# Layer 1 of a two-layer transformer pair: gate tiles as fp32 matmuls between the recurrent steps, first attention beside the recurrent weight tiles, 24 modulation dots at the output projections

## What is computed

```python
mod = silu(c) @ w_ada + b_ada                      # 6 vectors of 1024: sh1, sc1, gt1, sh2, sc2, gt2
xn = rms_norm(h, norm1_g) * (1 + sc1) + sh1
q, k, v, zrw, gate_logits = split(xn @ w_in)       # 512, 512, 512, 1792, 2048 columns
o_moba = attention(rope(rms_norm(q)), rope(rms_norm(k)), v)     # 8 heads of 64, causal
o_rwkv = rwkv7_time_mix(token_shift(zrw), ...)     # 8 heads of 64, recurrent over the tokens
g_moba, g_rwkv = split(sigmoid(gate_logits))
mixed = g_moba * (o_moba @ w_proj_moba) + g_rwkv * (o_rwkv @ w_proj_rwkv)
h = h + gt1 * (mixed @ w_out)
xn2 = rms_norm(h, norm2_g) * (1 + sc2) + sh2       # then peer_ffn(xn2), then layer 2
```

## Time and profile before

| | us |
|---|---|
| median of 3 runs | 1953.65 (1952.32 to 1954.14) |
| the profiled execution | 1950.17 |
| its span, first to last instruction | 1948.4 |
| `w_in`, split tiles | from 57.3 to 173 |
| attention of layer 1 ends | 194.4 |
| recurrent part ends, `proj` starts | 390.8 |
| `w_out` starts | 422.8 |

### The profile page before, as it was taken

The page is one execution under the profiler, slowest core; times in us unless marked ns, Lnnn a source line. Parts: engine busy times, 40 slices in busy tenths (PEclk is TensorE's granted clock), DMA queues, the critical chain, the costliest instruction groups (busy, mean ns, idle before and its releaser), DMA issues.

```text
span 1948.4 us, 30492 instructions
## 1 busy us (share of the span) xinstructions
PE 1723.4 (88%) x10498; PEld 1505.8 (77%) x10498; DVE 1355.6 (70%) x2735; ACT 740.4 (38%) x1289; POOL 91.9 (5%) x107
## 2 busy tenths in 40 slices
PE   2998378697997998899999999999799997879997
PEld 2997367586986776788888888888699855669997
DVE  6888855424599996678888888888444635448886
ACT  1454300102411334455555555555244214414443
POOL 0001100000000000000000000000005302200000
PEclk8999789898998998999999999999899997989999
DMA  9895000043464115777777777777354370025653
GB/s 337 286 322 175 0 1 1 1 120 118 148 188 146 41 55 170 219 227 239 237 233 238 235 239 234 237 233 226 127 178 152 116 246 1 9 91 183 183 182 108
DMA packets 101164, 315.66 MB, mean 162 GB/s; under 512 B 11232, under 2 KB 20448, under 8 KB 100576
## 3 DMA queue, kind: packets, MB, share of 16 engines
q1 hardware_dynamic: 100512, 311.07, 50.1%
q10 hardware_dynamic: 576, 3.59, 0.5%
HBM read 309.11 MB, written 5.51 MB: 161 GB/s over the span
## 4 chain that ended last, share of the span: by engine, by line
PE 65%; DVE 21%; issue 7%; ACT 4%; DMA 2%; POOL 1%; DVEq 0%; SPq 0%; ACTq 0%; POOLq 0%
PE bank L462 7%; PE bank L463 7%; PE bank L464 7%; PE bank L477 4%; PE bank L1509 4%; PE bank L1550 4%; PE bank L1552 4%; PE bank L1554 4%; PE bank L438 3%; ACT whi L451 3%; PE bank L478 2%; PE bank L488 2%; DVE wlo L456 2%; PE bank L1314 2%; DVE xn L1662 1%
## 5 line engine op out<-in xcount | busy, mean ns | idle before, releaser
L456 DVE TENSOR_TENSOR wlo<-wring,whi 128x1024 fp32r<-128x1024 f32 x364 | 443.5, 1224 | 126.0 <-ACT whi L451 116.4
L451 ACT CAST whi<-wring 128x1024 fp32r<-128x1024 f32 x380 | 396.8, 1046 | 72.5 <-PE bank L1554 49.0
L462 PE MATMUL bank<-xboth,whi 128*128 128x256 f32 x1088 | 311.9, 287 | 24.2 <-DVE wlo L456 22.0
L463 PE MATMUL bank<-xboth,whi 128*128 128x256 f32 x1088 | 309.7, 285 | 0.0
L464 PE MATMUL bank<-xboth,wlo 128*128 128x256 f32 x1088 | 309.6, 285 | 0.0
L477 PE MATMUL bank<-xboth,whi 128*128 128x512 f32 x658 | 235.8, 397 | 0.0
L462 PEld LDWEIGHTS bank<-xboth,whi 128*128 128x128 f32 x1088 | 210.8, 194 | 27.0 <-issue 23.9
L463 PEld LDWEIGHTS bank<-xboth,whi 128*128 128x128 f32 x1088 | 210.9, 194 | 0.5 <-issue 0.5
L464 PEld LDWEIGHTS bank<-xboth,wlo 128*128 128x128 f32 x1088 | 210.8, 194 | 0.0
L478 PE MATMUL bank<-xboth,wlo 128*128 128x256 f32 x658 | 184.5, 280 | 0.0
L1550 PE MATMUL bank<-whi,Whi 128*128 128x512 f32 x512 | 161.0, 396 | 15.2 <-DVE Wlo L1645 15.2
(11 more groups left out here) (362 smaller groups left out, 2790.7 us busy)
## 6 DMA issues: line engine op xcount, KB each, us to landing
wring<-in_w SPq DMA_DIRECT2D x463, 512.0 KB, 3.7
arena<-in_ada SPq DMA_DIRECT2D x48, 512.0 KB, 5.0
xn<-in_ada SPq DMA_DIRECT2D x96, 256.0 KB, 3.2
h_spill<-arena SPq DMA_DIRECT2D x34, 128.0 KB, 1.7
arena<-h_spill SPq DMA_DIRECT2D x34, 128.0 KB, 3.6
wring<-in_w SPq DMA_DIRECT2D x6, 384.0 KB, 3.1
wring<-in_w SPq DMA_DIRECT2D x9, 256.0 KB, 2.6
arena<-in_const ACTq DMA_DIRECT2D x1, 1200.0 KB, 5.1
```

The lines of the kernel that those rows point to most:

```text
L451: act.copy(whi[:, n % HSLOTS, :], wring[:, n % SLOTS, :]).then_inc(hi_ready, 1)
L456: eng.tensor_tensor(wlo[:, n % SLOTS, :], wring[:, n % SLOTS, :], whi[:, n % HSLOTS, :].bitcast(F32), ALU.subtract).then_inc(lo_ready, 1)
L462: pe.matmul(out, h, xh, start=start, stop=False, **kw)
L463: pe.matmul(out, h, xl, start=False, stop=False, **kw)
```

## The change

**Order of `w_in`.** The phase `w_in` has 26 tiles now: v, q and k, then the recurrent ones. The 16 gate tiles are a phase of their own, `gates1`, behind it, and are not split: `pe_gates1` multiplies a block of 128 x 128 by 256 tokens as one fp32 matmul, 128 of them in all, put between steps of the recurrent part; `act_gates1` takes the sigmoids there.

**Attention.** The three small steps stand behind tiles 12, 14 and 16. Attention starts behind tile 18, and each of its first seven turns is followed by one of the tiles 19 to 25 on PE, ACT and DVE. Its PSUM banks are 3 and 4 (scores), 5 and 6 (transposes) and 7 (values), one bank for values.

**Dots.** Eight dots stay in `w_in`. The other 24 are done one or two at a time behind each of the 16 tiles of `proj` and `w_out`, with five buffers of their own; SP issues their loads between those of the tiles.

```diff
-PHASES = [("w_in", 42), ("proj", 8), ("w_out", 8), ("wq", 16), ("peer", 2 * NK),
+PHASES = [("w_in", 26), ("gates1", 16), ("proj", 8), ("w_out", 8), ("wq", 16), ("peer", 2 * NK),
...
+        MOBA_BANKS, LAYER2_BANKS = ((3, 4), (5, 6), (7,)), ((0, 1), (3, 4), (6, 7))
...
             def values(j):
                 n, g = j["n"], j["group"]
                 pe.wait_ge(a_pt, n + 1)
-                if j["first"] and g >= 2:
-                    pe.wait_ge(a_free, g - 1)
+                held = len(j["banks"][2])
+                if j["first"] and g >= held:
+                    pe.wait_ge(a_free, g - held + 1)
...
+        dots_before = lambda j: min(max(3 * j // 2, 0), 3 * KT)
+        def sp_layer1_out(sp):
+            def ada(i):
+                if i >= BSLOTS:
+                    sp.wait_ge(ada_used, 3 * KT + i - BSLOTS + 1)
+                sp.dma_start(aringb[:, i % BSLOTS, :], a["ada"][3 * KT + i]).then_inc(blanded[i % BSLOTS], 16)
+            sp.wait_ge(t_new, 20)
+            for i in range(BSLOTS):
+                ada(i)
+            for j, n in enumerate(range(FIRST["proj"], FIRST["peer"])):
+                sp.wait_ge(tile_done, n - SLOTS + 1)
+                sp.dma_start(wring[:, n % SLOTS, :], a["w"][n]).then_inc(landed[n % SLOTS], 16)
+                for i in range(dots_before(j - SLOTS) + BSLOTS, dots_before(j - SLOTS + 1) + BSLOTS):
+                    if i < 3 * KT:
+                        ada(i)
...
-            ring_tiles_split(pe, "w_in", 4, MB_SUMS_AT)
+            ring_tiles_split(pe, "w_in", 4, 13)
             pe_moba_sums(pe)
-            ring_tiles_split(pe, "w_in", MB_SUMS_AT, MB_GIVE_AT)
+            ring_tiles_split(pe, "w_in", 13, 15)
             pe_moba_give(pe)
-            ring_tiles_split(pe, "w_in", MB_GIVE_AT, MB_ROT_AT)
+            ring_tiles_split(pe, "w_in", 15, 17)
             pe_moba_turn(pe)
-            ring_tiles_split(pe, "w_in", MB_ROT_AT, 42)
+            ring_tiles_split(pe, "w_in", 17, ATT_TILE - 3)
+            pe.wait_ge(mb_q, 3)
+            att_pe(pe, moba_jobs, beside=lambda t: t + ATT_TILE < COUNT["w_in"] and
+                   ring_tiles_split(pe, "w_in", t + ATT_TILE, t + ATT_TILE + 1))
+        ATT_TILE = 22
...
+            lo_tile(15)
+            dve_shift(dve, v, 1)
+            dve_moba_given(dve)
+            lo_tile(16)
+            dve_shift(dve, v, 2)
+            lo_tile(17)
+            dve_shift(dve, v, 3)
+            lo_tile(18)
+            dve_shift(dve, v, 4)
+            dve_moba_turned(dve, v)
+            lo_tile(19)
+            dve_shift(dve, v, 5)
+            att_dve(dve, v, moba_jobs, beside=beside)
...
+        def pe_gates1(pe, n0, n1):
+            for n in range(n0, n1):
+                t, k = divmod(n, KT)
+                tile, r = FIRST["gates1"] + t, RING0["gates1"] + t
+                if k == 0:
+                    pe.wait_ge(landed[tile % SLOTS], count_at(tile))
+                    pe.wait_ge(ring_free, r - BANKS + 1)
+                mm = pe.matmul(bank[r % BANKS][:, 0:S], blocks(tile % SLOTS, k), xn[:, k, :],
+                               start=(k == 0), stop=(k == KT - 1))
+                if k == KT - 1:
+                    mm.then_inc(tile_done, 1)
...
         def pe_rwkv(pe):
+            pe_gates1(pe, 0, 8)
             pe.wait_ge(lora_loaded, 16)
...
             mm.then_inc(rw_ss, 1)
+            pe_gates1(pe, 8, 48)
             pe.wait_ge(bd_ready, 1)
...
+            pe_gates1(pe, 48, 64)
             pe.wait_ge(t_init, 4)
...
                     product(n + 2)
+                if n < 16:
+                    pe_gates1(pe, 64 + n, 65 + n)
...
                 mm.then_inc(q_u, 1)
+                pe_gates1(pe, 80 + 6 * c, 82 + 6 * c)
                 pe.wait_ge(q_us, c + 1)
...
                 mm.then_inc(q_sa, 1)
+                pe_gates1(pe, 82 + 6 * c, 84 + 6 * c)
                 pe.wait_ge(q_sas, c + 1)
...
                 mm.then_inc(q_y, 1)
+                pe_gates1(pe, 84 + 6 * c, 86 + 6 * c)
...
             mm.then_inc(gn_ss, 1)
+            pe_gates1(pe, 104, 128)
...
+            act_gates1(act, 1, 6)
             act.wait_ge(bd_ready, 1)
...
+            act_gates1(act, 6, 10)
+            act.wait_ge(t_new, 20)
+            act.dma_start(rB["crow"], a["crow"][0:1, :].to_broadcast([P, D])).then_inc(crow_loaded, 16)
...
                 dve.tensor_tensor(mix1[:, m, :], mixt[:, m % 2, 0, :], mixt[:, m % 2, 1, :], ALU.add).then_inc(ring_free, 1)
+                dve_late_ada(dve, m)
...
-            dve_residual(dve, "w_out", 2)
+            dve_residual(dve, "w_out", 2, beside=lambda m: dve_late_ada(dve, KT + m))
             norm_squares(dve, nsq[1])
+            dve.wait_ge(ada_used, 6 * KT)
+            dve_add_bias(dve, v, 3 * KT, 6 * KT)
```

More of the change, by code:

```diff
@@ L53 @@
 WIDTH = {"cmp_w2": 512, "uq": 768, "uk": 512, "uv": 512}
-RINGED = ["w_in", "proj", "w_out", "wq", "w_in2", "uq", "uk", "uv", "w_o"]
+RINGED = ["w_in", "gates1", "proj", "w_out", "wq", "w_in2", "uq", "uk", "uv", "w_o"]
 RING0 = {}
@@ L548, in spans, with turns @@
             return CAUSAL if job["kind"] == "causal" else CMP
-        def turns(jobs, *stages):
+        def turns(jobs, *stages, beside=None):
             first, last = jobs[0]["n"], jobs[-1]["n"]
@@ L556, in turns, with score_bank, turn_bank, value_bank @@
                         stage(jobs[t + ahead - first])
-        def att_pe(pe, jobs):
+                if beside:
+                    beside(t - first)
+        MOBA_BANKS, LAYER2_BANKS = ((3, 4), (5, 6), (7,)), ((0, 1), (3, 4), (6, 7))
+        def score_bank(j):
+            return bank[j["banks"][0][j["n"] % 2]]
+        def turn_bank(j):
+            return bank[j["banks"][1][j["n"] % 2]]
+        def value_bank(j):
+            return bank[j["banks"][2][j["group"] % len(j["banks"][2])]]
+        def att_pe(pe, jobs, beside=None):
             def scores(j):
-                n, bk = j["n"], bank[j["n"] % 2]
+                n, bk = j["n"], score_bank(j)
                 if n >= 2:
@@ L596, in values, with att_act @@
                 mm.then_inc(a_out, 1)
-            turns(jobs, (3, scores), (0, turn), (-1, values))
-        def att_act(act, jobs):
+            turns(jobs, (3, scores), (0, turn), (-1, values), beside=beside)
+        def att_act(act, jobs, beside=None):
             def exps(j):
@@ L619, in copy, with att_dve @@
                 if j["kind"] == "causal":
-                    ins = act.copy(buf["pt"][:, o:o + 384], bank[3 + n % 2][:, 0:384])
+                    ins = act.copy(buf["pt"][:, o:o + 384], turn_bank(j)[:, 0:384])
                 else:
-                    ins = act.copy(buf["pt"][0:NCMP, o:o + 256], bank[3 + n % 2][0:NCMP, 0:256])
+                    ins = act.copy(buf["pt"][0:NCMP, o:o + 256], turn_bank(j)[0:NCMP, 0:256])
                 ins.then_inc(a_pt, 1)
-            turns(jobs, (2, exps), (0, copy))
-        def att_dve(dve, v, jobs):
+            turns(jobs, (2, exps), (0, copy), beside=beside)
+        def att_dve(dve, v, jobs, beside=None):
             def maxima(j):
@@ L655, in output @@
                     dve.wait_ge(a_out, j["n"] + 1)
-                    dve.tensor_copy(j["out"], bank[6 + j["group"] % 2][j["rows"], 0:S]).then_inc(a_free, 1)
-            turns(jobs, (3, maxima), (1, reciprocals), (-2, output))
+                    dve.tensor_copy(j["out"], value_bank(j)[j["rows"], 0:S]).then_inc(a_free, 1)
+            turns(jobs, (3, maxima), (1, reciprocals), (-2, output), beside=beside)
         def att_pool(pool, jobs):
@@ L673, in build_layer_pair @@
         qr = rM["qn"].rearrange("p (m t) -> p m t", m=8)
-        moba_jobs = [dict(n=h, group=h, first=True, last=True, kind="causal", scale=MD ** -0.5, gate=None,
+        moba_jobs = [dict(n=h, group=h, banks=MOBA_BANKS, first=True, last=True, kind="causal", scale=MD ** -0.5, gate=None,
                           q=[qr[:, h // 2, :]], k=[kz[:, h, :]], M=128, buf=att1,
@@ L841, in act_w_in @@
+        def act_w_in(act):
+            for t in range(ATT_TILE - 3):
+                act_w_in_tile(act, t)
+                if t == 12:
                     act_moba_roots(act)
+            act_lora(act)
+            att_act(act, moba_jobs, beside=lambda t: t + ATT_TILE < COUNT["w_in"] and act_w_in_tile(act, t + ATT_TILE))
         mb_sq, mb_ss, mb_rt, mb_qn, mb_rot, mb_q = (sem("mb_sq"), sem("mb_ss"), sem("mb_rt"), sem("mb_qn"),
@@ new lines, in dve_w_in @@
+            lo_tile(12)
+            squares(1)
+            dve.wait_ge(ada_used, 3 * KT)
+            dve_add_bias(dve, v, 2 * KT, 3 * KT)
+            lo_tile(13)
+            lo_tile(14)
+            dve_shift(dve, v, 0)
+            dve.wait_ge(mb_rt, 1)
+            dve.reciprocal(mrt[:, 0:S], mrt[:, 0:S]).then_inc(mb_inv, 1)
+            lo_tile(15)
[4 more added lines that the diff above has]
+            lo_tile(17)
@@ L1337, in dve_residual @@
                 ins.then_inc(ring_free, 1)
+                if beside:
+                    beside(m)
```

(6 more changed lines are left out.)

139 lines of the change are left out of this document (69 added, 70 removed).

## The result

The changed kernel takes 1906.9 us, the median of four runs from 1904.19 to 1915.75; the kernel before, run beside it, takes 1953.89 us. The ratio is 0.9766, with a 95% interval from 0.9737 to 0.9794: faster by 2.3%. The forecast was 1911 us and a range from 1902 to 1923. The profiled execution of the changed kernel took 1909.39 us, its span is 1907.56 us; before these were 1950.17 and 1948.38. So the two traces differ by 40.8 us.

A forecast was written before the change was run, and what follows sets the result against it. PE was taken to bound the first stage and the projections, and mostly to wait for DVE in the recurrent part. Terms -46.1 - 0.2 + 0.3 + 2.8 - 1.0 - 1.5 + 2.3 + 0.8 = -42.6 us gave 1911 us, range 1902 to 1923.

The forecast's parts named there:

- Gate tiles, removed: First stage: sixteen split gate tiles, 2.88 us apart on PE, leave the path: -46.1 us.
- Gate tiles, added: Recurrent part: 128 gate matmuls of 0.436 us, mostly hidden in PE's gaps; +0.3 ahead of lora products, +2.8 in chunks.
- Attention: Attention among split tiles: idle terms +1.1, +1.4, +2.2, +3.3; last turns end 8.6 us behind tile 25, attention at 147.6.
- Interleaving moves the idle time but hardly lessens it: Attention's turns between split tiles: 8.0 us idle against 8.2 before, -0.2 us.
- The fifth rival: Attention was to overlap, but the sum already has that at -0.2; only the gates pay. No chance listed.
- Dots: `proj` and `w_out`: dots hidden except the last two ahead of the norm's squares, +2.3 us; DMAs 0, at most +6.
- Clock: PE's clock behind shortened gaps: updates -1.0 us, `proj` -1.5, norm +0.8.
- the chained turns: Attention turns with tiles: waits on ACT or DVE hold up the next turn, +12 us, 1923; chance 0.13.
- rival 2: Clock at its upper end everywhere, first unit included, and half of attention's 8.0 us idle gone: -9 us, 1902; chance 0.13.

The follow-up runs named there:

- the block of gates: Changed kernel with all 128 gate matmuls and 16 sigmoids in one block ahead of the lora products, none in gaps, updates or chunks: 1958.92 us.
- DVE's output first: Changed kernel with DVE copying out head t-2's values ahead of, not behind, the maxima of head t+3 in the first attention: 1905.29 us, ratio 0.9744.
- three edits: Changed kernel with DVE copying values out ahead of the maxima, chunk gates moved into the two long gaps, and dots spread over `proj` and `w_out`: 1898.28 us, ratio 0.9707.

## Why the prediction was right

The mechanism of the gain, whole gate tiles moved into gaps that hold them, and most terms were as put, and the total of the traces is 1.8 us off. The terms of the clock are the weakest: they were choices between bounds, and one came out at nothing.

- *Gate tiles, removed*: the first scores came at 108.72 us, and 108.6 had been laid out. The 46.1 us hold.
- *Gate tiles, added*: the three long gaps took theirs for nothing, as the sums of busy and idle time show, and the block of gates confirms it from the other side. The updates still have a pitch of 3.49 us, with the matmul in the gap that was 0.58 us. The chunks cost +2.6 of the forecast 2.8, and moving their gates away gave 2.6 back.
- *Attention*: this is the step that was off, by 1.7 us against the sum (end at 149.83; the layout had 147.6, and the sum, which the layout doesn't quite meet, 194.4 - 46.1 - 0.2 = 148.1). The mechanism, values that wait for a copy behind the maxima, was named with 1.1 us in two turns; there are three, 1.09, 1.24 and 1.09 us. The third is in the tail (142.46), where the 8.6 us became 9.6. The two waits ahead were right: 0.85 us for the rest of tile 16, forecast 1.1, and 0.89 for `mb_q`, forecast 1.4.
- *"Interleaving moves the idle time but hardly lessens it"*: forecast -0.2, measured +1.5, in two terms of opposite sign. Without the gate tiles the kernel before would have its first scores at 176.53 - 46.1 - 7 x 2.88 = 110.3 us; they came at 108.72, so the covered rotation gave 1.6. From there attention's share is 41.11 - 7 x 2.88 = 20.95 us against 17.91, so 3.0 were lost, about the 3.2 that DVE's output first gives back. With that order, counted from the same first scores, attention ends 1.7 us earlier than in the kernel before less its gate tiles (194.4 - 46.1 = 148.3), nearly all of it by the rotation. The 4.2 us that interleaving is worth hold between kernels with one bank of values. The fifth rival's sentence, that only the gates pay, is true of the changed kernel.
- *Dots*: +2.2 us for two dots between the last addition and the squares, forecast 2.3, and they went when the two dots went. In the DMAs 0 held: 366 GB/s over 29 us without a wait of PE for a load. The Trainium skill (DMA: Bandwidth & Descriptors, Where 436 GB/s comes from) has about 358 GB/s as what binds transfers from HBM, worked out as half of a stack's rate for each of two cores. This trace, of a kernel on one core, exceeds it by 2%, so as a bound the figure didn't hold here; no term of the sum hung on it.
- *Clock*: `proj` gave -1.25 of -1.5, and the norm +0.6 of +0.8. That `proj` came so near is partly luck: behind the same wait of 2.85 us it took from 29.14 us (output first) to 32.13 (three edits) in other traces, against 32.04 before. The updates gave nothing of the -1.0: behind 3.48 us of waiting they began at a clock of 0.50. With 24 gates in that gap instead of 16 they began at 1.00 and gave 2.3 us, a little more than the bound of 1.9, which had only the first instruction in it. What failed here is the -1.0 put on a gap that is made shorter and not filled: in seven of eight traces it was worth nothing.

Of the rivals, the chained turns didn't come: turns with a tile are 3.5 to 6.0 us apart, as against a sum of parts of 11.5. The dense one (rival 2) isn't this kernel either, but the best variant has parts of it: the clock held in the units and the updates, not in `proj`, and the three waits in attention gone. Its price of -9 us was near: that kernel gained 11.9 and 13.5 us in its two traces up to the norm's end, 2.2 of them the dots and 2.6 the chunks, which the rival hadn't.

The median came out 4 us below the forecast, while the traces gained 1.8 us less than forecast. That is chance between executions, not a better forecast. The profiled execution of before is 3.5 us under its median (1950.17 to 1953.65), that of after 2.5 us over (1909.39 to 1906.9), and together these 6.0 us are the distance, but for 0.1. The spread of the repeats is large enough for it; where it arose in the executions that weren't profiled stays open.

## What to carry to other kernels

Work that depends on nothing late is best laid into gaps which end on another engine's own work: there its whole length was free here. Filled to within 1.1 us of its end, such a gap also went with a full clock behind it, in all three traces that had it so, while a gap filled in part left the outcome open (24 matmuls more in the two first gaps gave 2.6 us in the chunks that they left, and 4.5 us in stages where the clock was higher). When a buffer is taken away from a rotation, look at what stands ahead of its release on the releasing engine: one line's order on DVE was worth 3.2 us, and what the missing bank costs in the tail stayed. And judge edits of a few microseconds by the stages of two traces, since one kernel's total moved by over 10 us from execution to execution with the clock.

## What was not expected of the hardware

- The granted clock after a wait is not given by the wait's length. Behind 3.51 us of waiting it stayed at 1.00 before the change, behind 3.48 us it was 0.50 (the stretch from 224.1), behind 3.47 and 3.46 us the same kernel's first product took 2.05 and 3.78 us, and behind the same 2.90 us the same instructions took 3.72 us in one execution and 6.68 in another. The Trainium skill (TensorE: Matmul & The Clock Gate, Part 1) has the throttled clock as the default that activity releases; the direction agrees with the gates' effect, where idle times of 7.98 and 3.48 us reduced to 1.07 us and to nothing went with a clock of 1.00. As the prediction read it, all three filled gaps would end at full clock; in the changed kernel none did. The units began with 1.22 us for an instruction that takes 0.70 at full clock, the updates at 0.50, and `proj` at 0.50 too:

```profile
349.00:351.50 2.50, 2.48 (x6) 2.04 (x7) 0.00 (x0) 0.00 (x0) 0.00 (x0) 0.50 0.01 3
```

- The 16 inverse-update records took 3.78 us at half clock and 2.05 at full.
